# A decoder layer's two feature-wise layer norms made by halves of the tokens, with the output tiles in front of them

## What is computed

```python
h = layer_norm(alpha * h + 0.5 * swiglu(h, ffn1_...), ln1_g, ln1_b)      # pass 0
h = layer_norm(alpha * h + hybrid_mixer(h, ...),      ln2_g, ln2_b)      # pass 1
h = layer_norm(alpha * h + 0.5 * swiglu(h, ffn2_...), ln3_g, ln3_b)      # pass 2
return h[:, 16:]

def layer_norm(x, g, b):
    mu = mean(x); var = mean(square(x - mu))
    return (x - mu) * rsqrt(var + 1e-5) * g + b
```

## Time and profile before

| | us |
|---|---|
| median of 3 runs | 1118.2 |
| lowest, highest | 1115.24, 1118.43 |
| the profiled execution, its own time | 1114.91 |
| its span, first to last instruction | 1113.0 |
| TensorE busy | 1077.5 (97%) |
| VectorE, ScalarE, GpSimd busy | 466.9, 345.6, 129.5 |

### The profile page before, as it was taken

One profiled execution on the slowest core, in us unless ns is written; L12 is line 12 of the kernel. 1 busy time (PEld: TensorE's weight loads), 2 busy tenths in 40 slices (PEclk: granted clock), 3 DMA queues, 4 the chain that ended last, 5 costly groups with the idle time before them and its releaser, 6 DMA issues.

```text
span 1113.0 us, 16112 instructions
## 1 busy us (share of the span) xinstructions
PE 1077.5 (97%) x6635; PEld 933.9 (84%) x6635; DVE 466.9 (42%) x731; ACT 345.6 (31%) x452; POOL 129.5 (12%) x95
## 2 busy tenths in 40 slices
PE   8999999999999998999988999989999999999995
PEld 7999999999999997689865568768888888888885
DVE  4332332323232254689885533463232323232326
ACT  3322322222121234534337542353232323221211
POOL 5000000000011115212312103250000000000000
PEclk9999999999999999999998999999999999999998
DMA  6424233231322323122210101222424232143221
GB/s 192 114 76 112 75 93 96 75 101 52 105 79 78 115 76 97 39 77 77 77 38 1 39 1 38 76 76 76 113 75 112 76 109 80 52 142 104 78 78 75
DMA packets 159166, 90.35 MB, mean 81 GB/s; under 512 B 6596, under 2 KB 156792, under 8 KB 159128
## 3 DMA queue, kind: packets, MB, share of 16 engines
q1 hardware_dynamic: 159128, 89.83, 28.3%
HBM read 87.72 MB, written 2.10 MB: 81 GB/s over the span
## 4 chain that ended last, share of the span: by engine, by line
PE 88%; DVE 5%; ACT 3%; POOL 2%; issue 1%; DMA 0%; DVEq 0%; SPq 0%; POOLq 0%
PE ps L911 74%; PE ps L1081 4%; POOL xl L478 2%; PE ps L1355 2%; PE ps L1335 1%; PE ps L1346 1%; DVE x L1601 1%; PE ps L1363 1%; DVE sil L1595 1%; PE ps L1143 1%; ACT whi L606 1%; PE ps L1036 0%; PE ps L1035 0%; DVE x L1584 0%; PE ps L1037 0%
## 5 line engine op out<-in xcount | busy, mean ns | idle before, releaser
L911 PE MATMUL ps<-xl,whi 128*128 128x264 f32 (+1 forms) x1264 | 351.0, 330 | 8.9 <-POOL xl L478 8.0
L911 PE MATMUL ps<-xh,whi 128*128 128x264 f32 (+1 forms) x1264 | 355.8, 331 | 2.7 <-DVE wlo L1439 1.6
L911 PE MATMUL ps<-xh,wlo 128*128 128x264 f32 (+1 forms) x1264 | 352.8, 329 | 0.0
L911 PEld LDWEIGHTS ps<-xl,whi 128*128 128x128 f32 x1264 | 211.7, 189 | 36.4 <-POOL xl L478 16.1
L911 PEld LDWEIGHTS ps<-xh,whi 128*128 128x128 f32 x1264 | 212.5, 189 | 29.4 <-issue 5.2
L911 PEld LDWEIGHTS ps<-xh,wlo 128*128 128x128 f32 x1264 | 213.6, 189 | 22.2 <-issue 0.2
L1430 DVE TENSOR_TENSOR wlo<-wraw,whi 128x2048 fp32r<-128x2048 f32 (+1 forms) x81 | 171.6, 2118 | 144.0 <-ACT whi L606 144.0
L606 ACT ACTIVATE whi<-wraw 128x2048 fp32r<-128x2048 f32 (+1 forms) x89 | 152.4, 1712 | 129.6 <-PE ps L911 123.8
L1463 DVE TENSOR_TENSOR ht<-ps,sil 128x528 f32<-128x528 f32 (+1 forms) x44 | 30.8, 700 | 253.7 <-PE ps L911 247.4
L911 PE MATMUL ps<-hh,whi 128*128 128x264 f32 (+1 forms) x506 | 132.8, 319 | 0.0
L911 PE MATMUL ps<-hl,whi 128*128 128x264 f32 (+1 forms) x506 | 132.5, 318 | 0.0
(11 more groups left out here) (226 smaller groups left out, 921.2 us busy)
## 6 DMA issues: line engine op xcount, KB each, us to landing
wraw<-in_ffn_w_gate SPq DMA_DIRECT2D x44, 512.0 KB, 4.0
wraw<-in_ffn_w_up SPq DMA_DIRECT2D x43, 512.0 KB, 5.2
wraw<-in_ffn_w_down SPq DMA_DIRECT2D x32, 384.0 KB, 3.4
wraw<-in_ffn_w_down SPq DMA_DIRECT2D x32, 320.0 KB, 3.8
wraw<-in_w_in SPq DMA_DIRECT2D x19, 512.0 KB, 4.6
wraw<-in_w_out SPq DMA_DIRECT2D x8, 512.0 KB, 4.0
xin<-in_x SPq DMA_DIRECT2D x2, 1024.0 KB, 5.9
out<-zrow SPq DMA_DIRECT2D x8, 256.0 KB, 2.0
```

What stands on the lines that cost most here:

```text
L911: mm = pe.matmul(ps[:, b + e, 0:width], w, mov, start=(first and n == 0), stop=(last and n == 2))
```

## The change

Both normalisations by feature, and the last output tiles in front of them, are made by halves of the tokens (part e = 0 and 1: 264 each in pass 0, 256 each in pass 1).

- Pass 0: down tile 7 is made for the first half with all 22 hidden tiles, then for the second (`first_down_by_tokens`); the first half's `stats` stand inside the second half's products. Pass 1: the last unit of `w_out` (tiles 6 and 7) likewise (`last_out_by_tokens`), in banks 0 to 3.
- Residual, square, sums, statistics, variance, root, reciprocal, centre, multiply, both activations and `xl` are then made per half, so twice as many instructions at half the width. The second half's residual, statistics and variance stand between tiles of the first half in each queue.
- The inverse deviation goes to PSUM (banks 6 and 7, over the mean square) and not into `sil`.
- The first unit behind each normalisation does all tiles of half 0 and then those of half 1, with the second half's `stats` after its second tile. `keep_warm` goes there (it stays at the start of the kernel).
- Rounding and splitting of the mixer's unit 0 move into the first half's normalisation; unit 1 of the mixer, and of ffn 2, is rounded between the halves and split at the end. GpSimd sets the mixer's constants after its `xl` tiles.
- The mLSTM norm is made for all four blocks at once, with one root; numerators of block 4 stand in the middle of the last gate product, their copy before its sigmoid; heads 0 and 1 are normalised ahead of the attention, heads 2 and 3 after its first two scores.

```diff
+        def part(v, p, e):
+            return v[:, e * HT:(e + 1) * HT] if p == 0 else v[:, N_META + e * HALF_SEQ:N_META + (e + 1) * HALF_SEQ]
+        def part_bank(b, p, e):
+            return ps[:, b + e, 0:(HT, HALF_SEQ)[p]]
...
             def norm_lo(p):
-                for k in range(KT):
-                    x_lo(k, F[p]["aff_done"], k + 1, F[p]["split_done"], p)
+                for e in range(2):
+                    for k in range(KT):
+                        pool.wait_ge(F[p]["aff_done"], KT * e + k + 1)
+                        pool.tensor_tensor(part(xl[:, k, :], p, e), part(x[:, k, :], p, e),
+                                           part(xh[:, k, :], p, e).bitcast(F32), ALU.subtract).then_inc(F[p]["split_done"], 1)
...
# norm on ScalarE
+                if p == 1:
+                    square_part(KT - 2, 0)
+                square_part(KT - 1, 0)
+                mean_squared(0)
+                if p == 1:
+                    square_part(KT - 2, 1)
+                deviation(0)
+                if p == 0:
+                    hi(MIX0, 0, UW, False)
+                tiles(0, 0, 2)
+                square_part(KT - 1, 1)
+                tiles(0, 2, 5)
+                mean_squared(1)
+                tiles(0, 5, 6)
+                deviation(1)
+                tiles(0, 6, KT)
+                hi(MIX0 + 1 if p == 0 else UNIT0[2] + 1, 1, UW, True)
+                tiles(1, 0, KT)
...
# TensorE
+            def first_down_by_tokens(u):
+                for e in range(2):
+                    for half in range(2):
+                        pe.wait_ge(w_lo, u + (half + 1))
+                        for k in range(HALF_FT):
...
+                            if e == 1 and kk == 5:
+                                stats(0, 0)
+                        if e == 1:
+                            mm.then_inc(w_used, 1)
+                    if e == 0:
+                        mm.then_inc(F[0]["part_done"], 1)
...
+            def last_out_by_tokens():
...
+                for e in range(2):
+                    for c in range(2):
+                        for k in range(KT):
+                            mm = part_product((MIX0 + n) % 2, k * 256 + c * P, k, part_bank(2 * c, 1, e),
+                                              slice(N_META + e * HALF_SEQ, N_META + (e + 1) * HALF_SEQ))
+                            if (e, c, k) == (1, 0, 4):
+                                stats(1, 0)
...
             ffn(0)
-            stats(0)
-            keep_warm(WARM_NORM)
             mixer()
-            stats(1)
-            keep_warm(WARM_NORM)
             ffn(2)
...
-                o_half(19)
+                o_half(19, 0, 4)
                 numerators(4)
+                o_half(19, 4, KT)
                 lat_queries()
...
# norm on VectorE
+                if p == 1:
+                    residual_part(KT - 2, 0)
+                residual_part(KT - 1, 0)
+                variance(0)
+                if p == 1:
+                    residual_part(KT - 2, 1)
+                inverse(0)
+                tiles(0, 0, 2)
+                if p == 0:
+                    lo(MIX0, 0, UW)
+                residual_part(KT - 1, 1)
+                tiles(0, 2, 6)
+                variance(1)
+                tiles(0, 6, KT)
+                inverse(1)
+                tiles(1, 0, KT)
...
-                dve.reciprocal(var, flat(sil[:, 1, :], p)).then_inc(s["rstd_done"], 1)
+                    dve.reciprocal(part_bank(6, p, e), part(sil[:, 1, :], p, e)).then_inc(s["rstd_done"], 1)
...
# ScalarE, mixer
                 copy_num(3)
-                mlstm_sd(0, 3)
+                copy_num(4)
                 o_out(19)
-                copy_num(4)
+                mlstm_sd()
                 for h in range(ATT_H):
-                    if h == 4:
-                        mlstm_sd(3, 4)
```

More of the change, by code:

```diff
@@ L688, in norm, with square_part @@
                 s = F[p]
[L689 to L700, removed]
+                def square_part(m, e):
+                    act.wait_ge(s["z_done"], KT + e if p == 0 else m + 1 + 2 * e)
+                    act.wait_ge(s["sums_done"], m + 1)
+                    act.activation(part(sil[:, m % 2, :], p, e), part(x[:, m, :], p, e), ACT.Square).then_inc(s["sq_done"], 1)
@@ new lines, in mean_squared, with deviation, tiles @@
+                def mean_squared(e):
+                    act.wait_ge(s["stats_done"], 2 * e + 1)
+                    act.activation(part(sil[:, 0, :], p, e), part_bank(4, p, e), ACT.Square).then_inc(s["mu2_done"], 1)
+                def deviation(e):
+                    act.wait_ge(s["varc_done"], e + 1)
+                    act.activation(part(sil[:, 1, :], p, e), part(sil[:, 0, :], p, e), ACT.Sqrt).then_inc(s["sd_done"], 1)
+                def tiles(e, k0, k1):
+                    for k in range(k0, k1):
+                        act.wait_ge(s["norm_done"], KT * e + k + 1)
+                        if e == 0 and k == 0:
+                            act.wait_ge(vec_ready, 1)
+                        g, b = vec[:, V_G[p] + k:V_G[p] + k + 1], vec[:, V_B[p] + k:V_B[p] + k + 1]
+                        xk = part(x[:, k, :], p, e)
+                        act.activation(part(xh[:, k, :], p, e), xk, ACT.Identity, bias=b, scale=g).then_inc(s["hi_done"], 1)
+                        act.activation(xk, xk, ACT.Identity, bias=b, scale=g).then_inc(s["aff_done"], 1)
@@ L818, in mixer @@
                 attention()
-                for m in range(KT):
+                for m in range(KT - 2):
                     square(1, m, m % 2)
@@ L914, in _, with part_product @@
             X = (xh, xl)
+            def part_product(s, col, k, dst, tokens, passes=(0, 1, 2)):
+                w_h, w_l = whi[:, s, col:col + P], wlo[:, s, col:col + P]
+                a_h, a_l = xh[:, k, tokens], xl[:, k, tokens]
+                for n, (w, v) in enumerate(((w_h, a_h), (w_l, a_h), (w_h, a_l))):
+                    if n in passes:
+                        mm = pe.matmul(dst, w, v, start=(k == 0 and n == 0), stop=(k == KT - 1 and n == 2))
+                return mm
             def turn(k):
@@ new lines, in inverse, with tiles @@
+                def inverse(e):
+                    centre(e, 0)
+                    centre(e, 1)
+                    dve.wait_ge(s["sd_done"], e + 1)
+                    dve.reciprocal(part_bank(6, p, e), part(sil[:, 1, :], p, e)).then_inc(s["rstd_done"], 1)
+                    dve.wait_ge(s["rstd_done"], e + 1)
+                def tiles(e, k0, k1):
+                    for k in range(k0, k1):
+                        if 2 <= k + 1 < KT:
+                            centre(e, k + 1)
+                        dve.wait_ge(s["sub_done"], KT * e + k + 1)
+                        z = part(x[:, k, :], p, e)
+                        dve.tensor_tensor(z, z, part_bank(6, p, e), ALU.mult).then_inc(s["norm_done"], 1)
@@ L1764, in normed_mlstm @@
+                link(dve.tensor_tensor(mls[:, 2, :], mls[:, 2, :], mls[:, 1, :], ALU.mult))
+            def normed_mlstm(heads):
                 for h in heads:
-                    for j in range(j0, j1):
+                    for j in range(4):
                         q = h * 4 + j
```

196 lines of the change are left out of this document (111 added, 85 removed).

## The result

The changed kernel takes 1106.62 us (median of four runs, 1105.3 to 1106.95) against 1117.61 for the kernel before (four runs, 1115.24 to 1118.43): ratio 0.9911, 95% interval 0.9894 to 0.9929. The forecast was 1106. The profiled execution is shorter by 8.5 us only, 1104.5 for 1113.0, since before's profiled run lies 2.7 under its median of 1117.61 and after's only 0.3 under its own.

What follows compares the result with a forecast made beforehand. TensorE, busy 1077.5 of 1113.0 us, bounds the kernel; only its waits and low-clock work can be won. Span 1113.0 - 4.3 - 2.5 - 5.5 = 1100.7; median 1118.2 - 12.3 = 1105.9, say 1106 us; range 1099 to 1113 with rivals 1 and 2.

Steps and rivals of the forecast that it cites:

- the three signs that the prediction gave for being wrong: Affines over 0.7 us, clock rows falling to 0.5 at both first units, or attention ending less than 8 us earlier.
- the walk less its shift: Second ffn's first unit: last product near 737.4 us, less the shift of 9.8 before it.
- First normalisation, -4.3: Mixer's first unit behind the first normalisation: last product at 427.6 us against 431.9, so 4.3 us less.
- the stall: Inside the last down output: a new TensorE stall of 1.0 us, as VectorE splits the second weight half only at 392.67.
- the prices: Half-width pieces: products about 0.12 us, centre and multiply together 0.68 or 0.70, ScalarE activation 0.60 (0.51 to the next instruction).
- mLSTM norm, -5.5: mLSTM norm: no copy wait, second root or table load, third score masked 4.8 us earlier; 5.5 us less, bounds 3 and 7.
- Second normalisation, -2.5: Second ffn's first unit behind the second normalisation: last product at 737.4 us against 739.9, so 2.5 us less, without warming.
- a few cold us alone are absorbed in the pauses: Both first units: low clock costs time only once TensorE falls behind ScalarE's feed through most of them (1.4 against 1.0 per tile).
- the fourth rival: Both first units: without warming calls the clock holds at 1.2 GHz, +5 us, 1123 us; chance 0.05.
- Rivals 1 and 3: 1: ScalarE's fixed part costs, 0.65 for 0.51, 1112 us, chance 0.12. 3: halves overlap nothing, 1113 us, chance 0.04.
- Rival 2: Attention: the halves work but the mLSTM gain is lost there, -6.8, 1111 us; chance 0.12.
- at 0.73 for both activations: ScalarE in both normalisations: upper bound, half-width activations save nothing, sixteen pairs take 23.4 us, +4.3 us together.

Runs made afterwards that it cites:

- the repeat: The changed kernel run again with no edit: 1104.02 us, 0.9894 of the kernel before.
- the order alone: The kernel before with only the mLSTM part's new order, its norm still in two pieces and both normalisations whole and warmed: 1116.13 us, ratio 1.0006.
- before unwarmed: The kernel before without its two times 32 warming calls: 1116.23 us, ratio 0.9997.

## Why the prediction was right, and where not

The total was right, 1106 for 1106.6, by a sum in which two terms were off and two were missing: the medians differ by 11.0 us, the forecast by 12.3. That it came so near is in part luck: the second normalisation gave 2.3 us too little, and 1.1 more in the mLSTM norm (in executions without a cold spell there) and 1.1 in the second ffn, which no term had, made up for it. The two profiled executions differ by 8.5 only: after's has both cold spells of the middle columns. Two of the three signs that the prediction gave for being wrong came: the granted clock fell to 0.5 in both first units, and the last output units start 7.2 us earlier in the kernel after where it wanted at least 8 (9.6 in the repeat). The second ffn's first unit ends at 732.5, not at the 727.6 that the walk less its shift gave.

- **First normalisation, -4.3.** Measured -4.28 in the profile, and within 0.1 of it in four further kernels' executions; the stall, the prices and the feed came as walked. The clock fell here too, at 421 to 424, and here it was absorbed as the forecast said. It is not safe: where the clock fell near the end, in the kernel with the second norm whole, 1.5 of it was lost.
- **mLSTM norm, -5.5.** Mechanism right (the copy's wait alone gives nothing while the second root stays, as the order alone shows), size too small: -6.6, within the bounds of 3 and 7. The kernel before worked cold there (0.70 in the 590s); the walk mentioned the clock and put no price on it. The executions with a cold spell keep 5.0.
- **Second normalisation, -2.5.** This step failed: the stage gave 0.2 us in the profile after, and 0.3 to 0.6 against the same kernel with that normalisation whole. The sentence that failed is "a few cold us alone are absorbed in the pauses". The gap of 2.7 us without warming was foreseen, and its effect was only counted in the fourth rival, as an all-or-nothing case of slower products. Its real price, 1.7 to 2.0 us, came in two ways: through the second half's late statistics (0.5 us in the kernel after, all 1.7 in its repeat) and through a second fall on the last products (1.5 in the kernel after). Twelve calls bring it back, to 0.3 of the walked length. By the rule of the Trainium skill ("TensorE: Matmul & The Clock Gate", section "HAM oscillation — how this bites in real kernels") that idle gaps bring the clock down, this trace agrees, with a fall behind a wait of 2.82 us, as does that of the kernel before without its calls, behind one of 7.67; there the same fall cost 0.1 us, which the rule alone doesn't tell.
- **Given back between.** The forecast carried the 4.3 us unchanged to the attention. In the table's second column the kernel after loses 1.6 to a cold spell near 494; kernels with the old first normalisation lose it too in some executions (order alone 113.69, before unwarmed 113.61), so it is not a price of the change. Where that spell stays away, the new wait of 0.86 us near 525 and the fall behind it leave 0.9.
- **The second ffn** runs 1.1 us faster than in the kernel before (259.2 or 257.1 + 8 x 0.2325 = 259.0 for the same 1115 products, 260.4 before). Only the kernel before with and without its calls has the longer time; the one with the new order alone doesn't, though its ffn code is the same. Nothing in the trace names a cause, and it was not tried.
- **PSUM for the inverse deviation.** The multiplies are free of GpSimd in it, as charged. In SBUF a multiply would have taken 554 ns on average, not the 1251 of the whole tiles; by stage that kernel is some 2 us longer, the clock's falls in it, and by total time no difference is shown.
- Rivals 1 and 3 are out (595 ns; the first normalisation overlaps as walked). Rival 2 did not come: the attention kept the gain. Rival 4 was right in its mechanism and wrong in size. One sum of the prediction does not follow from its rows: at 0.73 for both activations sixteen pairs take 23.4 us for 16.3, 7.1 more in each normalisation, so the two together would be +7.4 and not +4.3; nothing hung on it, since the measured step is 0.50.

## What to carry to other kernels

When work is cut into halves, look for each new wait of TensorE and ask what stands behind it. A fall of the clock in the middle of tiles that another engine feeds cost nothing here; ahead of statistics that another engine needs, or on the last products of the unit, it cost 0.5 to 1.7 us. Fill such a wait where it is, not where the old one was: calls in front of products that are ready hold them up. An edit that takes away one wait can be worth nothing while the next one in the same queue stays. Compare executions by stage between fixed points, and first take out the stages that vary in repeats of one kernel.

## What was not expected of the hardware

The granted clock fell at different moments in executions of one kernel (710 to 714 and 728 to 731 in one, 707 to 714 and after 720 in the next), so that a spell of low clock sits on small products or passes them: 1.7 us each time. A wait as short as 0.86 us, behind two us of products of 4 rows and ahead of dense ones, was followed by a fall to about 0.5 in two executions, and the 120 products there took 1.6 us more; in the kernel after, without the wait, it stayed at 1.00 there. A wait of 1.97 us inside a fed unit was followed by a fall to 0.50 a microsecond after it. But 8 us at 0.50 under the slower feed of whole tiles cost 0.1, and 3 us in the middle of the half tiles nothing.
